# Two head norms of a hybrid decoder layer: factors folded in beforehand, and eight gate chunks moved into the second norm

## The reference, cut to what matters

```python
proj = h @ w_in                                   # ret, ssm, rwkv and gate columns
def head_norm(x, eps):
    mu = mean(x); xc = x - mu
    return xc * rsqrt(mean(xc * xc) + eps)
# RWKV-7 branch (16 heads of 64)
yr = head_norm(yr, RWKV_GN_EPS) * rwkv_lnx_g + rwkv_lnx_b
out_c = (yr + bonus) * g_rw
# retention branch (8 heads of 128)
out_a = silu(g_ret) * head_norm(o, RET_GN_EPS)
gates = sigmoid(gate_cols)
merged = sum_n gates[n] * (branch[n] @ w_branch[n])
```

## Time and profile before

| | us |
|---|---|
| median of 3 runs | 3430.93 (3430.68 to 3434.05) |
| the profiled execution, its own time | 3430.33 |
| its span, first to last instruction | 3428.7 |
| busy: PE, DVE, ACT, POOL | 3006.3, 1791.3, 1239.4, 516.6 |

### The profile page before, as it was taken

The page is one execution under the profiler, slowest core; times in us unless marked ns, Lnnn a source line. Parts: engine busy times, 40 slices in busy tenths (PEclk is TensorE's granted clock), DMA queues, the critical chain, the costliest instruction groups (busy, mean ns, idle before and its releaser), DMA issues. The chain is left out here.

```text
span 3428.7 us, 63556 instructions
## 1 busy us (share of the span) xinstructions
PE 3006.3 (88%) x25510; PEld 2751.0 (80%) x25510; DVE 1791.3 (52%) x2788; ACT 1239.4 (36%) x1663; POOL 516.6 (15%) x339
## 2 busy tenths in 40 slices
PE   8998898889887898799889998888898879977997
PEld 7997787677586897599889987876776868965997
DVE  4435635676575564344344356455855745644443
ACT  4435321044321443254254363210542224433442
POOL 0004530054210000000000055201443000000000
PEclk9999999899897999999989999999998979998998
DMA  4444330144273465344344444202353644644443
GB/s 161 147 136 140 109 89 3 30 120 164 81 272 148 129 198 171 142 134 148 111 139 150 136 135 117 63 3 49 101 182 93 242 171 122 203 147 148 147 147 102
DMA packets 119404, 448.15 MB, mean 131 GB/s; under 512 B 13616, under 2 KB 23888, under 8 KB 111632
## 3 DMA queue, kind: packets, MB, share of 16 engines
q1 hardware_dynamic: 97920, 329.75, 31.5%
q0 software_dynamic: 21264, 115.34, 9.1%
HBM read 397.01 MB, written 48.02 MB: 130 GB/s over the span
## 5 line engine op out<-in xcount | busy, mean ns | idle before, releaser
L1451 ACT ACTIVATE w_high<-ring 128x1024 fp32r<-128x1024 f32 x598 | 632.1, 1057 | 724.8 <-PE gemm_banks L855 345.5
L851 PE MATMUL gemm_banks<-in_high,w_high 128*128 128x320 f32 (+1 forms) x2864 | 852.3, 313 | 45.2 <-ACT w_high L1451 23.6
L852 PE MATMUL gemm_banks<-in_low,w_high 128*128 128x320 f32 (+1 forms) x2864 | 840.7, 309 | 0.0
L1827 DVE TENSOR_TENSOR w_low<-ring,w_high 128x1024 fp32r<-128x1024 f32 x436 | 532.4, 1221 | 504.6 <-ACT w_high L1451 504.1
L851 PEld LDWEIGHTS gemm_banks<-in_high,w_high 128*128 128x128 f32 x2864 | 544.6, 190 | 55.2 <-issue 36.8
L702 POOL TENSOR_TENSOR w_low<-ring,w_high 128x1024 fp32r<-128x1024 f32 x162 | 409.4, 2532 | 965.7 <-ACT w_high L1451 965.6
L852 PEld LDWEIGHTS gemm_banks<-in_low,w_high 128*128 128x128 f32 x2864 | 544.5, 190 | 2.7
L855 PE MATMUL gemm_banks<-in_high,w_low 128*128 128x320 f32 (+1 forms) x2864 | 473.8, 308 | 6.1 <-POOL w_low L702 3.9
L855 PEld LDWEIGHTS gemm_banks<-in_high,w_low 128*128 128x128 f32 x2864 | 429.8, 188 | 8.5 <-POOL w_low L702 4.9
L935 PE MATMUL gemm_banks<-act_high,w_high 128*128 128x320 f32 x704 | 215.2, 319 | 3.3 <-DVE arena L1876 3.3
L908 PE MATMUL gemm_banks<-in_high,w_high 128*128 128x320 f32 x640 | 206.4, 335 | 6.6 <-DVE arena L1926 4.0
(11 more groups left out here) (396 smaller groups left out, 4217.4 us busy)
## 6 DMA issues: line engine op xcount, KB each, us to landing
ring<-in_w SPq DMA_DIRECT2D x598, 512.0 KB, 3.6
arena<-in_kc POOLq DMA_DIRECT2D x16, 1024.0 KB, 6.8
arena<-in_vc POOLq DMA_DIRECT2D x16, 1024.0 KB, 9.1
out_fill<-stage SPq DMA_DIRECT2D x80, 160.0 KB, 3.9
arena<-out_fill POOLq DMA_DIRECT2D x4, 2560.0 KB, 11.0
arena<-in_ssm POOLq DMA_DIRECT2D x16, 512.0 KB, 12.8
out_s_ssm<-arena POOLq DMA_DIRECT2D x16, 512.0 KB, 13.7
arena<-in_ret POOLq DMA_DIRECT2D x16, 512.0 KB, 22.5
```

The costliest lines, as they stand in the source:

```text
L851: mm(dst, w_high[:, slot, w(k)], in_high[:, k, 0:n], start=(k == 0), stop=False)
L852: mm(dst, w_high[:, slot, w(k)], in_low[:, k, 0:n], start=False, stop=False)
L1451: f(w_high[:, slot], ring[:, s, 0:D], ACT.Copy).then_inc(weights_high, 1)
L1827: tt(w_low[:, slot], ring[:, pos % RING, 0:D], w_high[:, slot].bitcast(F32), ALU.subtract).then_inc(weights_split, 1)
```

## The change

RWKV norm: ahead of the recurrence DVE turns the bonus `rr` into (bonus + lnx_b) * g and the gate `rw_g` into lnx_g * g. After `centred` and the squares it forms LW = centred * rw_g. ACT writes the Exp into PSUM, over the sums. DVE multiplies LW by it out of PSUM, the last 512 columns first (new mark `tail`, for which PE now waits ahead of `ssm`), then the other 2,048, and adds rr.

Retention norm: the 8 gate chunks are computed by PE inside the norm, 3 after the first sums and 5 after the second, in the three `gp` banks that the sums leave. ACT copies them out unsquashed between its steps; one Sigmoid over all 2,560 columns follows after the activation of `ret_out` is rounded (`gate(0)`). DVE splits the gate weights ahead of, between and after its products. The arena places of the three gates change; the reload of the third gate is a DMA of its own, issued after `("ret", "done")`, ahead of those of the ssd branch, x and the memory.

```diff
-        gates = R(3, KT, T)
+        gates_at = R.at
+        gates = [split(arena[:, gates_at + j * KT * T:gates_at + (j + 1) * KT * T], KT, T) for j in (1, 2, 0)]
+        R(3, KT, T)
...
-                pool.dma_start(gates[:, 1:3].rearrange("p a b t -> p (a b) t"),
-                               outs["fill"][:, 3 * KT:5 * KT]).then_inc(dma["gates_back"][0], 16)
+                pool.dma_start(gates[1], outs["fill"][:, 3 * KT:4 * KT]).then_inc(dma["gates_back"][0], 16)
                 arrived(pool, l, "stored", n)
                 pool.wait_ge(hn_v.sem, hn_v.value[("ret", "done")])
+                pool.dma_start(gates[2], outs["fill"][:, 4 * KT:5 * KT]).then_inc(dma["gates_back"][0], 16)
...
+            def gate_chunks(start, end):
+
+                for c in range(start, end):
+                    pos = BASE["gates"] + c
+                    pe.wait_ge(weights_high, RANK[pos] + 1)
+                    pe.wait_ge(psum_free, RING + (pos - 2 if c >= 3 else BASE["gates"]))
+                    slot, dst = RANK[pos] % AHEAD, gate_bank(c)
+                    for k in range(KT):
+                        w = slice(k * P, (k + 1) * P)
+                        mm(dst, w_high[:, slot, w], in_high[:, k], start=(k == 0), stop=False)
+                        mm(dst, w_high[:, slot, w], in_low[:, k], start=False, stop=False)
+                    pe.wait_ge(weights_split, RANK[pos] + 1)
...
             def headnorm(tag, src, sq, table):
                 tile_sums(hn_p, (tag, "mean"), K(table), src)
                 if tag == "rw":
                     fill("fill_rwkv", 1)
+                else:
+                    gate_chunks(0, 3)
                 need(hn_a, (tag, "sq"))
                 tile_sums(hn_p, (tag, "var"), K(table), sq)
+                if tag == "ret":
+                    gate_chunks(3, KT)
...
-                need(hn_a, ("rw", "root"))
+                need(hn_v, ("rw", "tail"))
...
-                need(hn_a, ("ret", "root"))
...
-                projection("gates")
...
+            def rw_headnorm(sq, root, eps):
+                need(hn_v, ("rw", "centred"))
+                A_.mark(f(sq, hsrc["rw"], ACT.Square), hn_a, ("rw", "sq"))
+                nc.scalar.preload_act_table_set("natural_log_exp_and_others")
+                fill("fill_rwkv", 1)
+                need(hn_p, ("rw", "var"))
+                (b0, b1), (r0_, r1_) = sum_spans(), spans(root)
+                A_(f(r0_, b0, ACT.Ln, bias=eps, scale=1.0 / hsize["rw"]))
+                A_(f(r1_, b1, ACT.Ln, bias=eps, scale=1.0 / hsize["rw"]))
+                A_(f(b0, r0_, ACT.Exp, scale=-0.5))
+                A_.mark(f(b1, r1_, ACT.Exp, scale=-0.5), hn_a, ("rw", "root"))
+                fill("fill_rwkv", 4)
+
+            def ret_headnorm(sq, root, eps):
+                gate_weights(2)
+                need(hn_v, ("ret", "centred"))
+                A_.mark(f(sq, hsrc["ret"], ACT.Square), hn_a, ("ret", "sq"))
+                nc.scalar.preload_act_table_set("natural_log_exp_and_others")
+                for c in range(3):
+                    gate_copy(c)
+                    if c < 2:
+                        gate_weights(c + 3)
+                need(hn_p, ("ret", "var"))
                 for dst, src in zip(spans(root), sum_spans()):
-                    A_(f(dst, src, ACT.Ln, bias=eps, scale=1.0 / hsize[tag]))
...
+                    A_(f(dst, src, ACT.Ln, bias=eps, scale=1.0 / hsize["ret"]))
+                gate_weights(5)
+                A_.mark(f(root, root, ACT.Exp, scale=-0.5), hn_a, ("ret", "root"))
+                for c in range(3, KT):
+                    gate_copy(c)
+                    if c + 3 < KT + AHEAD:
+                        gate_weights(c + 3)
...
                 need(hn_v, ("ret", "done"))
-                merge_gates()
                 high_parts("ret", ra)
+                gate(0)
                 stream("ret_out")
...
                 V_.mark(nc.vector.memset(S, 0.0), pre_v, "done")
+                for i in range(KT):
+                    V_(stt(rr[:, i], rr[:, i], PR("lnx_b", i), rw_g[:, i], ALU.add, ALU.mult))
+                for i in range(KT):
+                    V_(ts(rw_g[:, i], rw_g[:, i], PR("lnx_g", i), None, ALU.mult))
...
-                headnorm("rw", Bt, E3, C64)
-                for i in range(KT):
-                    V_(ts(Bt[:, i], Bt[:, i], PR("lnx_g", i), PR("lnx_b", i), ALU.mult, ALU.add))
-                V_(tt(Bt, Bt, rr, ALU.add))
-                V_.mark(tt(rc, Bt, rw_g, ALU.mult), hn_v, ("rw", "done"))
+                centre("rw", Bt, C64)
+                need(hn_a, ("rw", "sq"))
+                V_(tt(LW, Bt, rw_g, ALU.mult))
+                need(hn_a, ("rw", "root"))
+                (b0, b1), (v0, v1) = sum_spans(), spans(LW)
+                V_.mark(tt(v1, b1, v1, ALU.mult), hn_v, ("rw", "tail"))
+                V_(tt(v0, b0, v0, ALU.mult))
+                V_.mark(tt(rc, LW, rr, ALU.add), hn_v, ("rw", "done"))
...
-                headnorm("ret", ra, hroot, P)
+                centre("ret", ra, P)
+                low = lambda c: weights(0, RING, BASE["gates"] + c)
+                for c in range(2, 6):
+                    low(c)
+                need(hn_a, ("ret", "root"))
+                V_(tt(ra, ra, hroot, ALU.mult))
+                low(6)
                 V_.mark(tt(ra, ra, qkvg[:, 24:32], ALU.mult), hn_v, ("ret", "done"))
-
-            def gate_weights():
...
+                for c in range(7, KT + AHEAD):
+                    low(c)
...
-                    if j:
-                        need(gate_open, j)
+                    need(gate_open, j)
```

More of the change, by code:

```diff
@@ L583, in build @@
         hn_a = marks("headnorm_scalar", [(t, k) for t in hn for k in ("sq", "root")])
-        hn_v = marks("headnorm_vector", [(t, k) for t in hn for k in ("centred", "done")])
+        hn_v = marks("headnorm_vector", [("rw", "centred"), ("rw", "tail"), ("rw", "done"), ("ret", "centred"), ("ret", "done")])
         cv_v = marks("conv_filtered", list(range(CB)))
@@ L995, in tile_sums @@
                 hit(ins_, marks_, name)
+            def gate_chunks(start, end):
[9 more added lines that the diff above has]
+                    pe.wait_ge(weights_split, RANK[pos] + 1)
+                    for k in range(KT):
+                        w = slice(k * P, (k + 1) * P)
+                        ins_ = mm(dst, w_low[:, slot, w], in_high[:, k], start=False, stop=(k == KT - 1))
+                        if k == 0:
+                            ins_.then_inc(high_used, 1)
+                    ins_.then_inc(chunk_done, 1)
             def headnorm(tag, src, sq, table):
@@ L1564, in rwkv_columns, with gate_weights @@
                     weights(0, RING, SPLIT[RANK[b] + c + AHEAD])
-            def headnorm(tag, sq, root, eps):
-                need(hn_v, (tag, "centred"))
-                A_.mark(f(sq, hsrc[tag], ACT.Square), hn_a, (tag, "sq"))
-                nc.scalar.preload_act_table_set("natural_log_exp_and_others")
-                if tag == "rw":
-                    fill("fill_rwkv", 1)
-                need(hn_p, (tag, "var"))
-                for dst, src in zip(spans(root), sum_spans()):
-                    A_(f(dst, src, ACT.Ln, bias=eps, scale=1.0 / hsize[tag]))
-                A_.mark(f(root, root, ACT.Exp, scale=-0.5), hn_a, (tag, "root"))
-                if tag == "rw":
-                    fill("fill_rwkv", 4)
+            def gate_weights(c):
+                weights(0, RING, BASE["gates"] + c)
@@ new lines, in gate_copy @@
+            def gate_copy(c):
+                act_.wait_ge(chunk_done, BASE["gates"] + c + 1)
+                f(gates[0][:, c], gate_bank(c), ACT.Copy).then_inc(psum_free, 1)
+            def rw_headnorm(sq, root, eps):
+                need(hn_v, ("rw", "centred"))
+                A_.mark(f(sq, hsrc["rw"], ACT.Square), hn_a, ("rw", "sq"))
+                nc.scalar.preload_act_table_set("natural_log_exp_and_others")
+                fill("fill_rwkv", 1)
[6 more added lines that the diff above has]
+                fill("fill_rwkv", 4)
@@ L1704, in retention @@
                     A_.mark(f(vtk[0:n, tb, 512:1024], bank(7)[0:n, 0:512], ACT.Copy), A, ("tr", tb))
[L1705 to L1715, removed]
+                ret_headnorm(hsq, hroot, K("eps")[:, 1:2])
             def gate(j):
-                A_.mark(f(gates[:, j], gates[:, j], ACT.Sigmoid), gate_open, j)
+                A_.mark(f(gates[j], gates[j], ACT.Sigmoid), gate_open, j)
             def attention():
@@ L1944, in chunks64, with centre @@
                 return v.rearrange("p a (c t) -> p a c t", t=C64)
-            def headnorm(tag, src, root, n):
+            def centre(tag, src, n):
                 need(hn_p, (tag, "mean"))
@@ L2314, in retention @@
                         only(j + 2)
-                headnorm("ret", ra, hroot, P)
+                centre("ret", ra, P)
[5 more added lines that the diff above has]
+                low(6)
```

(5 more changed lines are left out.)

15 lines of the change are left out of this document (7 added, 8 removed).

## The result

The changed kernel takes 3380.97 us (median; 3377.91 to 3386.19), the kernel before, on the same chip, 3432.26 (3430.68 to 3434.05). The ratio is 0.9852, with an interval of 0.9835 to 0.9869: 51 us less. The forecast was 3378.5. The profiled execution is the longest of those: 3386.19 us, with a span of 3384.6.

A forecast was written before the change was run, and what follows sets the result against it. PE, busy 88%, was taken to lose time to pauses in the retention norm and to DVE's pace in ssm. 9.7 - 0.2 + 16.7 = 26.2 us a layer, 52.4 for two, from 3430.93 gave 3378.5; range 3367 to 3397.

The forecast's parts named there:

- Part 3: Retention norm: gate chunks fill PE's pauses, 15.8 us less plus 0.9 at the seam; 16.7 a layer, bounds 13 to 17.2.
- Part 2: Ahead of the recurrence: sixteen added DVE operations hidden in 46.7 us of idle time; cost 0.2 us a layer, bounds 0 to 1.5.
- Part 1: RWKV norm's end: less vector work behind the root starts the ssm stage earlier; 9.7 us a layer, bounds 5 to 14.5.
- `done` at 714 to 719: RWKV norm's end: the three operations left behind the root take 5.7 to 9.8 us, in place of 24.5 until L2075 ends.
- ACT empties chunk 0 at 725.6 to 726.1: Start of ssm: ACT empties ssm chunk 0 right after chunk 3's `w_high`, rather than from 732.8 to 733.35.
- `rw_saved` at 722.35: Start of ssm: POOL raises this after splitting ssm chunk 1; DVE's edge terms then start 10.4 us earlier than 732.8.
- The edge terms take 2.7: Start of ssm: DVE's edge terms run from 722.35 to 725.0, with the duration they had before, 735.46 - 732.8.
- rival A: ssm stage: POOL's splits and DVE's operations meet more often, eating most of the 9.7; 3396 us; chance 0.12.
- Rival B: Retention norm: ACT's strict order holds Ln or Exp, PE pauses at chunk 5, clock falls; 7 us a layer, 3392; chance 0.09.
- Rival C: Gates and `ret_out`: weights arrive late, making it slower than before; at 20 us landing 16 a layer more, 3462; chance 0.03.
- Rival D: Start of ssm: ACT waits for the saves behind `rw_saved`, not `done`, so only part 3 counts; 3398; chance 0.06.
- four signs named for a wrong prediction: PE waiting over 1 us for POOL before the recurrence; `ret_out` ring waits; longer small ssm DVE operations; `L2109` not 9 us earlier.

The follow-up runs named there:

- wait_root: Changed kernel, but PE waits for the retention norm's root before gate chunk 3, with chunk 5's weights and split behind the root; 3397.10 us, ratio 0.9891.
- prep_triple: Changed kernel with the sixteen early operations ahead of the recurrence done three times, twice into a tile nobody reads; 3393.66 us, ratio 0.9878.
- dve_splits: Changed kernel, but DVE itself splits ssm chunks 0 to 2 around the edge terms and POOL starts with chunk 3; 3387.29 us, ratio 0.9872.
- best: `dve_splits`, but ACT empties ssm chunk 0 before chunk 3's `w_high`, and DVE splits the last fill chunk before the bonus sum; 3377.17 us, ratio 0.9838.
- rw_only: The kernel before with the RWKV norm's change alone; 3422.11 us, ratio 0.9963.

## Why the prediction was right, point by point

**What bounds the kernel** held. The gain came from exactly the two places named, and the second one, where PE paused, gave nearly three quarters of it.

**Part 3** was right to 0.2 us in layer 1. From the end of the first sums to the end of the last gate chunk the prediction had 32.6 us and the trace has 32.4 (1068.8, i.e. 1062.29 + 5.61 + two matmuls, to 1101.2, i.e. 1102.48 - 1.28). The seam is 0.9 shorter as said (2.19 to 1.28), the norm 16.9 in all against 16.7. Layer 2 had 58.9 before and has 40.9, 18.0 less. Over all traces of the study the stretch takes 57.1 to 58.9 in the old form (mean of four 58.0) and 39.7 to 40.9 in the new one (mean of fourteen 40.5). So the term is 17.5 a layer, 0.8 above the value I took and 0.3 above its bound: I had read it from one layer, whose stretch happened to be the shortest of the four. The schedule behind it held too. The Exp began at 1087.3, 25.0 us behind the first sum (predicted 1094.2 - 1068.9 = 25.3), and no wait of PE above 1 us is left between the sums and the rounding. `wait_root` shows what this cover is worth: 7.5 us in each layer. The step at the narrowest margin was the Sigmoid, hidden with 0.5 us to spare by the prediction and with 0.36 in the trace.

**Part 2** was right: 0.2 us, no wait of PE for POOL. The worst case of 27.5 us for sixteen operations was 18.4. `prep_triple` shows that they are free only because of the cover.

**Part 1 is the term that was mis-sized:** 9.7 us a layer expected, 6.3 found. Its steps, one by one:
- `done` at 714 to 719: right, 715.1. The two products out of PSUM take 2.98 together as from their row, and POOL's split, which runs beside the larger of them from 710.01, doesn't lengthen it (2.29, as the operation of the same size out of PSUM takes at 1068.87, L1992, with no split beside it). The Trainium skill says in the GPSIMD Engine Reference, 1. Specifications, that GpSimd contends with VectorE when that has two SBUF inputs or runs in a 2-port mode. The trace agrees: the product with one operand in PSUM isn't slowed, the sum with both in SBUF is (3.45 against 2.82 alone).
- ACT empties chunk 0 at 725.6 to 726.1: right, 725.92.
- `rw_saved` at 722.35: wrong. The trace has DVE starting at 720.52. The mark is raised while POOL's split of 720.35 is still running, not at its end. By itself it would have gained nothing: by the prediction's own times DVE had to wait for ACT until 726.1 either way.
- The edge terms take 2.7: wrong, and this is the step that failed. They take 8.7 us (720.52 to 729.18), since three of them lie under a running split. I had the duration from a row in which they fell between splits, and counted a possible meeting with splits in the bounds only, though it put their start at 722.35, on the end of the first split of the pair at 719.92, whose second runs from there to 724.79 by the earlier trace rows: the meeting was certain.
- The wait of PE for POOL's first split "may go, or stay": it stayed, 1.13 us, one split later, beside the bonus sum.

DVE's time-step work so starts at 729.18 instead of 726.1, 3.1 us later than forecast, and the rest of the stage follows: the last convolution and ssd moved by 6.3 as well. That is rival A's mechanism (splits and DVE operations meet), at one place, taking a third of the 9.7 (with the 0.3 or so that stayed with PE's wait); the rest of the stage lost nothing, DVE being busy 48.55 us of 54 against 48.62. The bounds of 5 to 14.5 held it. Short edge terms alone would not have given the 9.7: `dve_splits` has them and gains 7.1, since a second meeting that the sum hadn't counted either lay under the first, the time-step work beside the split of chunk 3 (2.28 us for an operation that takes 0.32 alone). With both gone `best` has 10.1, but this doesn't confirm the 9.7: there ACT also empties chunk 0 some 5 us earlier than the prediction's limit of 726.1.

Rival B is refuted by the trace and priced by `wait_root`. Rival C: weights are waited for by ACT, twice by about 2 us, and PE has them in time. Rival D falls with `rw_only`. Of the four signs named for a wrong prediction three are in the trace, waits for the ring in `ret_out` (ACT's only), longer small DVE operations, and the old L2109 less than 9 us earlier; the last two are the mis-sized term.

**The sum.** The terms as measured give 2 x (6.3 - 0.2 + 17.5) = 47.2, and at the norm ahead of layer 2's attention the trace shows 47.9. The medians say 51.3, and 47.3 beside the second set of kernels. The forecast of 52.4 was 3.4 too high in one term and 0.8 too low in the other, a layer. Executions of one kernel differ by some 8 us, part of which lies in attention, as the 3.8 us given back there shows; so the nearness of 3378.5 to 3380.97 is partly luck. Where that variation comes from stays open; no run was made for it.

## What to carry to other kernels

When a wait is removed, look at what the work behind it will then run beside, not only at when it starts: a row of a small operation's duration holds only for its old neighbours, and if its new start is another engine's mark, see what that engine runs right behind the mark. Put independent matrix work into both gaps of a norm (sums, root) and check the narrowest cover on each in-order engine; this gave 17.5 us a layer. Where freeing one delay gives next to nothing, look for a second that lies beside it (0.7 to 0.8 us a layer by either of two edits, 3.8 with all of them).

## What the runs showed of the hardware

- A DVE operation of 96 to 288 columns with two SBUF inputs, 0.28 to 0.46 us alone, took 2.30 to 2.55 us when it started beside a POOL split (2.41 alone), and ended 0.1 to 0.2 us after it. The same happens to a scaling of 16 x 320 with one input, 0.31 alone and 2.15 to 2.28 then. A large DVE operation with both inputs in SBUF slows POOL more than itself: two splits, the second beside the bonus sum, took 7.34 us in `dve_splits`, one alone 2.41, while the sum took 3.45 instead of 2.82. The times fit turns rather than a shared pace: the first split ends at 708.34 + 2.41 = 710.75, the sum, begun at 710.00, is over 2.7 us later at 713.45, and the second split 2.2 us after that at 715.68. Where one split ends and the next begins within the pair is worked out here, not shown.
- POOL's mark behind a split was seen by DVE 0.17 us after the split began, 2.3 us before its end.
- Exp of 2,560 columns in two halves into PSUM took 1.88 + 0.60, against 2.34 in one piece into SBUF: 0.14 more.
- Ten matmuls of 512 columns took about 4.5 us (3.59 for the eight) without a pause before them, and 6.41 for the eight behind a pause of 5.61; the mean granted clock of the norm's stretch was 0.95 against 0.87, between the two levels of 1.2 and 2.4 GHz.
